# Gated delta heads: decay rows by DMA broadcast from a scratch, and the output sum moved in the product order

## What is computed

```python
gc = jnp.cumsum(g, axis=-1)
diff = gc[..., :, None] - gc[..., None, :]
gamma = jnp.where(incl, jnp.exp(jnp.where(incl, diff, 0.0)), 0.0)
m = jnp.where(strict, jnp.einsum('nbhid,nbhjd->nbhij', kb, k) * gamma, 0.0)
t_inv = lax.linalg.triangular_solve(eye + m, eye, left_side=True, lower=True)
w_c = t_inv @ (kb * jnp.exp(gc)[..., None])
u_c = t_inv @ (v * beta[..., None])
qk = jnp.einsum('nbhid,nbhjd->nbhij', q, k) * gamma
qg = q * jnp.exp(gc)[..., None]
# scan over the chunks: v_new = u - w s;  o = qg s + qk v_new;  s = s exp(g_end) + kd' v_new
o = rms_norm(o, onorm_g) * jax.nn.silu(z)
```

## Time and profile before

| what | value |
|---|---|
| median of 3 runs | 3049.18 us |
| lowest, highest | 3046.46, 3049.21 us |
| the profiled execution | 3048.8 us |
| its span in the profile | 3047.1 us |
| mean granted clock of TensorE | 0.987 |
| TensorE busy | 2947.9 us, 97% |
| VectorE, ScalarE, GpSimd busy | 1046.3, 721.5, 221.6 us |

### The profile page before, as it was taken

How to read it: one execution, slowest core, us unless ns; L and a number is a source line. 1 busy time by engine, 2 the same in 40 slices (tenths; PEclk the granted TensorE clock), 3 DMA queues, 4 the chain that set the end, 5 groups by cost and what they waited for, 6 DMA issues and landing times.

```text
span 3047.1 us, 41455 instructions
## 1 busy us (share of the span) xinstructions
PE 2947.9 (97%) x16894; PEld 1700.0 (56%) x16894; DVE 1046.3 (34%) x2033; ACT 721.5 (24%) x1405; POOL 221.6 (7%) x280
## 2 busy tenths in 40 slices
PE   5999999999999999999998999999999989999998
PEld 2777776777444443444443557765555544675443
DVE  3555554554212224545512125531101222552011
ACT  3344443333200002121101225630000022462000
POOL 0222211112000000000000101000000001100000
PEclk9999999999989999999999999999999999999999
DMA  5000000010424342444322211001111113101222
GB/s 199 22 29 23 29 29 29 23 29 31 151 96 138 124 130 97 145 158 149 128 84 67 80 42 42 2 16 54 49 53 50 48 42 93 49 1 49 76 76 76
DMA packets 59847, 214.07 MB, mean 70 GB/s; under 512 B 6401, under 2 KB 8577, under 8 KB 59442
## 3 DMA queue, kind: packets, MB, share of 16 engines
q1 hardware_dynamic: 42512, 153.11, 15.7%
q0 software_dynamic: 13344, 50.59, 4.9%
q10 hardware_dynamic: 3842, 8.19, 0.7%
HBM read 208.20 MB, written 2.10 MB: 69 GB/s over the span
## 4 chain that ended last, share of the span: by engine, by line
PE 92%; DVE 3%; ACT 2%; DMA 1%; issue 1%; POOL 0%; ACTq 0%; DVEq 0%; SPq 0%
PE psum L361 89%; PE psum L728 3%; DVE arena L1353 1%; DMA arena<-in_ctxT 1%; DVE arena L1336 0%; DVE arena L1333 0%; POOL arena L1763 0%; ACT arena L968 0%; DMA arena<-in_stream 0%; ACT L987 0%; DVE arena L1359 0%; DVE arena L1341 0%; ACT arena L916 0%; ACT arena L992 0%; PE psum L555 0%
## 5 line engine op out<-in xcount | busy, mean ns | idle before, releaser
L361 PE MATMUL psum<-arena 64*64 64x64 f32 (+6 forms) x16094 | 2853.7, 361 | 86.4 <-ACT arena L916 18.9
L361 PEld LDWEIGHTS psum<-arena 128*128 128x128 f32 (+4 forms) x16094 | 1613.4, 162 | 1308.1 <-issue 1130.3
L1463 DVE SCALAR_TENSOR_TENSOR arena<-arena 128x1024 f32<-128x1024 f32 x128 | 149.2, 1220 | 4.9 <-DMA arena<-in_mods 4.7
L1708 DVE SCALAR_TENSOR_TENSOR arena<-arena,psum 128x512 f32<-128x512 f32 x32 | 21.2, 684 | 371.8 <-PE psum L361 371.8
L1133 ACT ACTIVATE arena<-psum,arena 128x512 f32<-128x512 f32 (+2 forms) x160 | 115.1, 727 | 30.6 <-DVE arena L1620 17.6
L1187 ACT ACTIVATE arena<-psum 128x512 f32<-128x512 f32 x32 | 19.1, 597 | 372.5 <-PE psum L361 372.5
L1582 DVE COPY arena<-psum 128x512 f32<-128x512 f32 x26 | 18.0, 691 | 238.5 <-PE psum L361 238.5
L728 PE MATMUL psum<-arena 128*128 128x128 f32 x704 | 94.5, 280 | 4.1 <-ACT arena L1133 4.0
L728 PEld LDWEIGHTS psum<-arena 128*128 128x128 f32 x704 | 76.5, 141 | 29.0 <-ACT arena L1133 14.8
L1777 POOL DMA_DIRECT2D arena<-in_mods x76 | 40.1, 528 | 689.7 <-DVE arena L1463 689.7
L1783 POOL DMA_DIRECT2D arena<-in_bias x16 | 8.7, 550 | 1109.7 <-DVE arena L1592 848.3
(11 more groups left out here) (206 smaller groups left out, 1328.6 us busy)
## 6 DMA issues: line engine op xcount, KB each, us to landing
arena<-in_stream SPq DMA_DIRECT2D x288, 512.0 KB, 3.6
arena<-in_mods POOLq DMA_DIRECT2D x80, 512.0 KB, 3.6
arena<-in_bias POOLq DMA_DIRECT2D x16, 384.0 KB, 3.8
arena<-in_xT ACTq DMA_DIRECT2D x1, 2048.0 KB, 17.7
out<-arena SPq DMA_DIRECT2D x1, 2048.0 KB, 7.2
arena<-in_conds ACTq DMA_DIRECT2D x1, 1536.0 KB
arena<-arena POOLq DMA_DIRECT2D x4, 384.0 KB, 4.3
arena<-in_ctxT ACTq DMA_DIRECT2D x1, 1024.0 KB, 19.9
```

Source lines behind the costliest of these rows:

```text
L361: return pe.matmul(out, lhsT, rhs, start=start, stop=stop, skip_group_check=True)
L1463: m = stt(mjunk[:, b % 2, :] if x < len(conds) - 1 else slot, slot, 0.5, cb[:, c, :], ALU.mult, ALU.mult, accum_out=dst(x))
```

## The change

The gate sums are transposed once, to partitions 0 to 15. ACT copies them to `gcT` (two copies instead of four), POOL stores `gcT` to a scratch in DRAM (`gc_rows`, 16 rows of 768), waits for that to land, and loads the two rows of head 0 onto all 128 partitions (`decay`, four slots of 768: two heads by two directions; 384 KB a load). At the start of its part of head i it issues the two loads of head i + 1. `gm`, `head_decays`, `decay_rows` and the semaphore R of the matmuls are gone. ACT makes `eR` with one Exp over 1536 elements out of SBUF, and does it behind Square of k instead of ahead of Tanh. DVE reads the 12 differences from `decay` in SBUF. On PE the q product starts right behind the output product of the head before; after its first two steps stands `out_sum`, now into bank 5, and then the other six steps.

```diff
+        gc_rows = nc.dram_tensor("gc_rows", (2 * HEADS, TOK), F32).ap()
...
-        gm = hp.take(TOK)
+        decay = hp.take(4, TOK)
...
+            return flat(decay[:, 2 * (i % 2):2 * (i % 2) + 2, :])
...
             for c in range(CH):
-                for r in (0, 32):
-                    m = mm(psum[r:r + 16, 2 if c >= XC else 5, (c % 4) * P:(c % 4 + 1) * P], gt[:, 1, c, :], ident)
+                m = mm(psum[0:16, 2 if c >= XC else 5, (c % 4) * P:(c % 4 + 1) * P], gt[:, 1, c, :], ident)
...
-                mm(psum[:, 4, :], ones, osq).then_inc(s("osum"), 1)
+                mm(psum[:, 5, :], ones, osq).then_inc(s("osum"), 1)
 
             for i in range(HEADS):
 
-                pe.wait_ge(s("gm"), i + 1)
-                for d in range(2):
-                    decay_rows(i, d, False).then_inc(s("R"), 1)
-                decay_rows(i, 0, True).then_inc(s("R"), 1)
                 if i:
+                    steps(T_HEAD + 1, range(0, 2), 4, None, i)
                     out_sum(i - 1)
-                pe.wait_ge(s("R"), 4 * i + 3)
-                decay_rows(i, 1, True).then_inc(s("R"), 1)
-                if i:
-                    pe.wait_ge(s("oln"), i)
-                    steps(T_HEAD + 1, range(KT), 4, None, i)
+                    steps(T_HEAD + 1, range(2, KT), 4, None, i)
...
-                pe.wait_ge(s("E"), 3 * i + 3)
...
                 centre(0, cbk, 0, 1, 0)
-                act.wait_ge(s("R"), 4 * i + 4)
-                f(eR[:, 0, 0:SEQ], psum[:, 2, :], ACT.Exp)
-                f(eR[:, 1, 0:SEQ], psum[:, 5, :], ACT.Exp)
-                f(eR[:, :, SEQ:TOK], psum[:, 3, :].rearrange("p (d c) -> p d c", d=2), ACT.Exp).then_inc(s("eR"), 1)
                 half_silu(0, sk, cbk)
                 act.wait_ge(s("silu"), 4 * i + 1)
                 f(sqk, sk, ACT.Square).then_inc(s("squares"), 1)
+                act.wait_ge(s(f"R{i % 2}"), 32 * (i // 2 + 1))
+                f(flat(eR), decays(i), ACT.Exp).then_inc(s("eR"), 1)
...
-                dve.wait_ge(s("eR"), i + 1)
-                for g, bank in enumerate((2, 5, 3)):
+                dve.wait_ge(s(f"R{i % 2}"), 32 * (i // 2 + 1))
+                for g in range(3):
...
-                        m = ts(E[:, 4 * g + t, :], psum[:, bank, t * P:(t + 1) * P], sc[:, 1, c, d:d + 1], 0.0,
-                               ALU.add, ALU.min)
+                        m = ts(E[:, 4 * g + t, :], decay[:, 2 * (i % 2) + d, coff(c):coff(c) + P], sc[:, 1, c, d:d + 1],
+                               0.0, ALU.add, ALU.min)
...
-                    elif l == 4:
-                        head_decays(i + 1)
...
+            def load_decays(i):
+
+                if i >= 2:
+                    pool.wait_ge(s("Et"), 3 * (i - 2) + 3)
+                    pool.wait_ge(s("eR"), i - 1)
+                for d in range(2):
+                    row = HEADS * d + i
+                    pool.dma_start(decay[:, 2 * (i % 2) + d, :], gc_rows[row:row + 1, :].to_broadcast([P, TOK]))\
+                        .then_inc(s(f"R{i % 2}"), 16)
+
+            pool.wait_ge(s("Tz"), 4)
+            pool.wait_ge(s("gcTs"), 1)
+            pool.dma_start(gc_rows, gcT[0:16, :]).then_inc(s("gc_out"), 16)
+            pool.wait_ge(s("gc_out"), 16)
+            load_decays(0)
             for i in range(HEADS):
 
+                if i < HEADS - 1:
+                    load_decays(i + 1)
```

More of the change, by code:

```diff
@@ L326, in chunk_at, with decays @@
             return 2 * SEQ * a + c * P if c < XC else SEQ + CTX * a + (c - XC) * P
+        def decays(i):
+            return flat(decay[:, 2 * (i % 2):2 * (i % 2) + 2, :])
         def slot2(j):
@@ L448, in _ @@
             pe.wait_ge(s("gates"), 1)
-            pe.wait_ge(s("Tz"), 5)
+            pe.wait_ge(s("Tz"), 4)
             def next_k(n, i):
@@ L949, in _ @@
             act.wait_ge(s("gcum"), 2)
[L950 to L953, removed]
+            f(gcT[0:16, 0:SEQ], psum[0:16, 5, :], ACT.Copy)
+            f(gcT[0:16, SEQ:TOK], psum[0:16, 2, 0:CTX], ACT.Copy).then_inc(s("gcTs"), 1)
             for i in range(HEADS):
@@ L1036, in _ @@
                 act.wait_ge(s("osum"), i + 1)
-                f(orn, psum[:, 4, :], ACT.Ln, scale=1.0 / P, bias=vec("eps")).then_inc(s("oln"), 1)
+                f(orn, psum[:, 5, :], ACT.Ln, scale=1.0 / P, bias=vec("eps")).then_inc(s("oln"), 1)
                 act.wait_ge(s("oln"), i + 1)
@@ L1316, in _ @@
             dve.wait_ge(s("gates"), 1)
-            dve.wait_ge(s("gcTs"), 2)
             gAf = gA.rearrange("p k c n -> p (k c n)").rearrange("p (m h) -> p m h", h=HEADS)
-            def head_decays(i):
-                ts(gm[0:48, :], gcT[0:48, :], con1[0:48, bass.ds(CON1["sel"] + i, 1)], None, ALU.mult).then_inc(s("gm"), 1)
-            head_decays(0)
             for i in range(HEADS):
@@ L1743, in _ @@
             pool.dma_start(con1, a_con1).then_inc(s("small"), 16)
-            pool.memset(gcT[0:64, :], 0.0).then_inc(s("Tz"), 1)
             for g in range(3):
```

## The result

The changed kernel takes 3053.16 us, median of 17 runs (3045.72 to 3055.57), beside 3047.20 for the kernel before in its 17 runs on the same chips (3042.48 to 3049.28). The ratio is 1.0018, with a 95% interval of 1.0011 to 1.0025: some 5.5 us slower. The forecast was 1.3 us faster, inside 3042 to 3054. The time lies inside the range, but it moved to the other side, and clear of the noise of these many runs, though by less than the 0.2% that the forecast had called measurable.

A forecast was written before the change was run, and what follows sets the result against it. Two chains were taken to bound the kernel side by side: TensorE's work and the output-sum-to-`kk` chain over ACT and DVE. From 3048.8, -3.4 - 0.35 + 2.5 gave 3047.55, plus 0.4 for the median: 3047.9 us, range 3042 to 3054.

The forecast's parts named there:

- The view and the question: Seam between heads: TensorE's work and the ACT/DVE chain end nearly together; 20.6 us leaving TensorE come back as waits.
- Square starts 0.43 us earlier: Heads 1 to 7: two q steps (1.72 us) replace 2.15 us of products ahead of `out_sum`, so Ln through Square start earlier.
- The Exp of 1536: Between Square of k and the Exp of `E`: takes 1.49 us, 1.38 of it adding to the chain.
- net 0.05 gain: Heads 1 to 7: L1333 and `kk` come 0.05 us earlier a head, 0.35 in seven.
- The clock: TensorE's 3.0 us idle ahead of the sums lowers the clock in five of seven heads, 0.5 us each: +2.5 us.
- The sum's step: Clock falls in heads 1 to 7 meet sums and v product; after 0.9 to 1.2 us spare, 0.4 to 0.7 remain.
- Rival (c): Heads 1 to 7 from `kk` on: the clock fall lasts into the first level, 1.63 us each, 3056.9; chance 0.09.
- Head 0: Decay rows through DRAM, store 3.0 us and loads 4.8, bring Ln to 87.45 against 90.86: -3.4 us.
- the sum's 81.3: Head 0: the decay rows land at 73.5 + 3.0 + 4.8 = 81.3 us.
- What costs nothing: Loads of heads 1 to 7 (4.8 us, issued over 85 us ahead), `head_decays` and banks 4 and 5 add no time.

The follow-up runs named there:

- e3: The kernel before, with both directions' decay products taken from partitions 0 to 15 (output wrong, work the same): ratio 1.0026, 3056.89 us.
- e10: The changed kernel with GpSimd's masking waiting for all three groups of DVE's differences, nothing else: 3056.55 us in one run.
- e1: The changed kernel with the Exp of 1536 ahead of the Tanh of k in heads 1 to 7, not behind the Square: ratio 1.0033, 3058.18 us.
- e8: e6 with the first step of the v product moved ahead of the sums of k's squares in heads 1 to 7: ratio 0.9954, 3037.27 us.
- e6: e1 with GpSimd's masking waiting for all three groups of differences and the output sum behind one q step instead of two: ratio 0.9980, 3044.32 us.
- e9: e8 with five useless products of 512 columns ahead of `kk` in head 0: ratio 0.9952, 3032.55 us.
- e2: The changed kernel with three useless 128x512 products behind the q product of heads 1 to 7: ratio 1.0006, 3049.14 us.
- e7: e6 with two useless 512-column products behind q in heads 1 to 7 and five ahead of `kk` in head 0: ratio 0.9947, 3033.12 us.

## Why the prediction was wrong, step by step

**The view and the question: right.** There are two chains with nearly the same end, TensorE's own work and the chain over ACT and DVE, and the first one's 20.6 us are not the gain: TensorE's idle of 3.0 us ahead of the sums was forecast, 3.1 came, seven times.

**"Square starts 0.43 us earlier": wrong.** This is the largest of three misses (3.2, 2.9 and 2.4 us), each of which was enough to turn the sign of a forecast of -1.25. The step set the pieces of the decay rows end to end, 2.15 us, against 1.72 for two q steps. The line of pieces in the earlier trace rows is for products over all partitions; those of 16 partitions in two different groups of 32 overlapped, and the real figure was 1.7. Output Square to Ln went from 2.55 to 2.58, and e3 shows the overlap by taking it away (3.40). The miss is 7 x 0.46 = 3.2 us.

**The Exp of 1536: right.** 1.47 us against 1.49; the chain from Square to k grew by 0.37 where the step has 0.38 (its net 0.05 gain is this less the 0.43). Nothing else of this part moved.

**The clock: right in kind, too small in size.** Five falls at 0.5 us were forecast, 2.5; six came and cost 5.4. Four of them cost 0.27 to 0.52 us, as reckoned. Heads 2 and 6 cost 1.8 each. TensorE in head 2:

```profile
255.10 12.36 PE L366 MATMUL psum<-arena 128*128 128x512 f32 x36 [3.10 <-ACT arena L961]
```

Sums, v product and `kk` follow each other there without a wait, in 12.36 us; in head 1 they take 8.03 + 0.91 of waiting + 1.60 = 10.54. The clock was down from before the sums until 261.2: 6.1 us of work at half speed, 3.0 us late, of which the spare 0.9 to 1.2 before `kk` covers a part; 1.82 is left. In heads 3, 4, 5 and 7 the stretches at 0.50 add up to 3.4 us, 1.7 late, less the same cover: 0.5. The sum's step knew only this second kind, a stretch of 3.4 us; the stretches of heads 2 and 6 last 6.8. Rival (c), put at 0.09, had the other price (1.63), but at another place (from `kk` on), where no fall came. The error was to treat the price as one number. All this is read from the profiled execution.

**Head 0: -3.4 forecast, -1.9 at `kk`, -1.0 at the output product.** The lines:

```profile
73.25 0.52 POOL L1737 DMA_DIRECT2D gc_rows<-arena  x1 [68.85 <-ACT arena L940]
...
75.53 2.17 POOL L1732 DMA_DIRECT2D arena<-gc_rows  x4 [1.76 <-DMA gc_rows<-arena]
...
81.20 3.54 DVE L1332 TENSOR_SCALAR arena<-arena 128x128 f32<-128x128 f32 x12 [3.32 <-DMA arena<-gc_rows]
...
83.29 2.61 POOL L1747 TENSOR_TENSOR arena<-arena 128x512 f32<-128x512 f32 x2 [5.59 <-ACT arena L967]
...
84.67 0.74 DVE L1312 SCALAR_TENSOR_TENSOR arena<-psum,arena 128x511 f32<-128x511 f32 x1
...
91.14 2.93 PE L366 MATMUL psum<-arena 128*128 128x128 f32 x12 [5.40 <-DVE arena L1338]
```

The store took 2.0 us from issue to landing and not 3.0, but the loads were landed 5.67 behind their first issue and not 4.82; the rows came at 81.2, which is 82.0 on the time of the trace before, against 81.3. For the store, an estimate of 2.1 us from the formula that the prediction takes from the Trainium skill, "DMA: Bandwidth & Descriptors", section "Anatomy of one DMA — SWDGE (gpsimd) path", was nearer; its estimate for the landing of the rows, 79.5, was further off than the sum's 81.3. Then the differences took 3.54 us, because one of them met the masking (e10), and q's taps started another 0.8 later than reckoned. That leaves -1.9 at `kk`. Another 0.9 us went between there and the output product. The clock was down from 90.5 to 97.3, around the whole of `kk` and the work behind it, and in the trace before only from 94.0 to 97.4, beginning with `kk`; that fits, but no run separates it from the walk, which varies by itself.

**What costs nothing: right**, for the loads of heads 1 to 7 (no wait on them in the trace), `head_decays` and the banks: an undisturbed head takes 63.57 us from M to the Square of its output in both kernels. That differences out of SBUF can be blocked by GpSimd was missing; it decided e1.

By the profiled executions the miss is 7.3 us, from -1.25 to +6.0. In it are 3.2 of the overlap (-0.35 forecast, +2.8 come), 2.9 of the clock and 2.4 in head 0, less the 0.8 of the earlier start and the 0.2 elsewhere in the heads: 7.5. The decay rows took 0.4 us more than two products side by side and one of 256 columns (0.86 + 0.43). By the starts of the single pieces this is four times 0.1 us, at the two changes between products over 128 and over 16 partitions; the reason stays open. So does what decides at which moment of the same 3.1 us of idle the clock falls or whether it does (head 1 kept it), and why the stretch between M and the output product, the levels and the walk over the chunks, takes 0.2 to 1.7 us more than 63.57 in some of heads 1 to 6 of every kernel, and 0.5 to 3.4 more in head 0.

## What to carry to other kernels

Before you count removed TensorE work as gain, see who releases the engine next; and when its products use few partitions, take their time from the distance between their neighbours, not from the sum of pieces. If TensorE is made to wait, put some of its own later work into the gap: here one v step ahead of a wait, a reordering of lines, brought 0.26% (e8 against e6), as much as useless products did. An elementwise instruction moved from PSUM to SBUF gets faster alone (0.28 us against 0.34) but begins to compete with GpSimd, so look at what GpSimd does in the same microseconds.

## What the runs showed of the hardware that was not expected

- Products over 16 partitions in different groups of 32 (0 to 15, 32 to 47) ran side by side: taking both from partitions 0 to 15 made the same three products ahead of the output sum 0.85 us longer (e3).
- The clock fell in e3 at about 251.8 us with TensorE busy by the trace and no wait over 0.2 us; from 247.2 on it had run decay products over 16 partitions, one behind another, and the output sum. Falls came at five of e3's seven seams. In the kernel before, with the same products side by side, the clock stayed at 1.00 at all seven. That the order of these products is the reason is not shown further.
- A fall of the clock cost between 0 and 1.8 us of a head, by what TensorE did meanwhile: nothing where it had others to wait for afterwards (e1: falls in six of heads 1 to 7, "k to M" at 2.66 in five of them), up to 1.8 where it became the pace.
- Equal idles did not end equally: 3.10 us ahead of the sums left the clock at 1.00 in head 1 and took it to the 1.2 GHz level in heads 2 to 7; two idles of 1.05 and 1.09 us (e9) never did.
- Useless work on TensorE can pay: e2 runs 2.6 us of it in each of seven heads and is faster than the changed kernel by 0.12%, with intervals that just overlap; e7 runs 1.7 us of it in seven heads and 4.3 in head 0 and is faster than e6 by 0.33%.
